# Two transformer blocks in one kernel: attention maps added before they are divided, bias rows of the modulations first, one more weight slot in two expert stages, SSD decays with their step in the exponent

## The reference, cut to what matters

```python
# first block, for layer in (0, 1)
mod = silu(c) @ ada_w[layer] + ada_b[layer]            # shift, scale, gate, twice
h = rms_norm(x, g) * (1 + sc1) + sh1
# layer 0: HGRN branch and differential attention; layer 1: windowed attention
#   differential: a1, a2 = softmax(q1 k1), softmax(q2 k2)
#   y = rms_norm((a1 - lam * a2) @ v) * (1 - lambda_init)
x = x + g1 * y
x = x + g2 * routed_moe(h2, ...)                       # 16 experts, top 2
# second block
acum = cumsum(dt * a)                                  # within chunks of 128 tokens
y_diag = einsum(cb, exp(acum_t - acum_s) * lower, x * dt_s)
states = einsum(bm, exp(acum_end - acum) * dt, x)      # forwards and backwards
y_off = einsum(cm, exp(acum), h_prev)
# then Fourier branch, gates, output product, rms_norm
ffn = expert_choice_ffn(h, ...)                        # 16 experts, 32 tokens each
```

## Time and profile before

| | us |
|---|---|
| median of 3 runs | 2982.18 (2977.14 to 2983.55) |
| the profiled execution | 2980.63 |
| its span in the profile | 2979.2 |

### The profile page before, as it was taken

The page is one execution under the profiler, slowest core; times in us unless marked ns, Lnnn a source line. Parts: engine busy times, 40 slices in busy tenths (PEclk is TensorE's granted clock), DMA queues, the critical chain, the costliest instruction groups (busy, mean ns, idle before and its releaser), DMA issues.

```text
span 2979.2 us, 30705 instructions
## 1 busy us (share of the span) xinstructions
PE 2396.1 (80%) x12449; PEld 1451.7 (49%) x12449; DVE 1295.0 (43%) x2115; ACT 968.8 (33%) x1492; POOL 108.7 (4%) x177
## 2 busy tenths in 40 slices
PE   5967696869999999698487777759888987778776
PEld 3733474658888887443232222228666762222222
DVE  2276638469999998354200000024685351000001
ACT  3344324348888787233100000034234340000000
POOL 1000300010000000100100000000000000000000
PEclk8978798879999999799799999979999998999999
DMA  9267650169999996664699999963103428999997
GB/s 346 93 228 279 204 215 1 58 245 388 395 393 395 392 385 250 242 245 167 225 398 398 401 402 401 406 229 114 57 1 119 171 89 340 409 409 409 409 410 287
DMA packets 246855, 819.48 MB, mean 275 GB/s; under 512 B 11075, under 2 KB 11241, under 8 KB 246448
## 3 DMA queue, kind: packets, MB, share of 16 engines
q1 hardware_dynamic: 226688, 753.88, 65.7%
q0 software_dynamic: 14432, 45.54, 4.5%
q10 hardware_dynamic: 5584, 17.98, 1.5%
HBM read 779.46 MB, written 37.90 MB: 274 GB/s over the span
## 4 chain that ended last, share of the span: by engine, by line
PE 58%; DMA 25%; DVE 10%; issue 3%; ACT 2%; SPq 1%; POOL 1%; DVEq 0%; PEldq 0%; ACTq 0%; POOLq 0%
PE PS L253 55%; DMA ring<-in_moe_w_up 8%; DMA ring<-in_w_e_down 5%; DMA ring<-in_moe_w_gate 4%; DMA ring<-in_w_e_up 3%; DMA ring<-in_w_e_gate 2%; PE PS L1824 1%; DVE hgrn L964 1%; DMA ring<-in_moe_w_down 1%; SPq L390 1%; DMA ring<-in_ada_w 1%; PE PS L566 1%; DVE SM L2460 0%; DMA row<-YP,DST 0%; DMA SM<-in_router_w 0%
## 5 line engine op out<-in xcount | busy, mean ns | idle before, releaser
L426 DVE TENSOR_TENSOR cut<-ring,cut 128x1024 fp32r<-128x1024 f32 x492 | 584.3, 1221 | 261.8 <-ACT cut L418 250.2
L418 ACT CAST cut<-ring 128x1024 fp32r<-128x1024 f32 x492 | 508.8, 1053 | 348.6 <-PE PS L253 321.7
L253 PE MATMUL PS<-cut,xeT 128*128 128x512 f32 x1536 | 366.1, 395 | 3.3 <-DVE cut L426 3.2
L253 PEld LDWEIGHTS PS<-cut,xeT 128*128 128x128 f32 x1536 | 286.7, 189 | 68.3 <-DVE cut L426 6.3
L253 PE MATMUL PS<-ring,hidT 128*64 128x512 f32 (+1 forms) x1024 | 242.4, 623 | 71.2 <-DMA ring<-in_w_e_down 33.5
L253 PE MATMUL PS<-ring,xeT 128*64 128x512 f32 x1024 | 239.0, 614 | 72.4 <-DMA ring<-in_moe_w_gate 38.1
L253 PE MATMUL PS<-ring,XE 128*32 128x512 f32 x1008 | 235.6, 621 | 62.9 <-DMA ring<-in_w_e_up 40.9
L253 PE MATMUL PS<-cut,parts 128*128 128x512 f32 x864 | 210.4, 406 | 24.5 <-DVE cut L426 14.8
L253 PE MATMUL PS<-parts,cut 128*128 128x512 f32 x864 | 204.2, 396 | 3.6 <-DVE cut L426 3.6
L253 PEld LDWEIGHTS PS<-cut,parts 128*128 128x128 f32 x864 | 168.5, 196 | 67.6 <-issue 18.7
L253 PEld LDWEIGHTS PS<-ring,xeT 128*64 128x64 f32 x1024 | 76.2, 140 | 234.0 <-issue 169.8
(11 more groups left out here) (539 smaller groups left out, 2494.0 us busy)
## 6 DMA issues: line engine op xcount, KB each, us to landing
ring<-in_moe_w_gate SPq DMA_DIRECT2D x64, 2048.0 KB, 12.8
ring<-in_moe_w_up SPq DMA_DIRECT2D x64, 2048.0 KB, 12.2
ring<-in_moe_w_down SPq DMA_DIRECT2D x64, 2048.0 KB, 12.2
ring<-in_w_e_up SPq DMA_DIRECT2D x32, 2048.0 KB, 18.6
ring<-in_w_e_down SPq DMA_DIRECT2D x32, 2048.0 KB, 20.0
ring<-in_w_e_gate SPq DMA_DIRECT2D x31, 2048.0 KB, 19.8
ring<-in_ada_w SPq DMA_DIRECT2D x24, 2048.0 KB, 9.2
ring<-in_w_in SPq DMA_DIRECT2D x13, 2048.0 KB, 7.5
```

Of the source, the lines that this page charges most:

```text
L253: return pe.matmul(o, l, r, start=start, stop=stop, **kw)
L418: act.copy(self.bufs[i % len(self.bufs)][0], w).then_inc(self.high.sem, 1)
L426: dve.tensor_tensor(low, w, high.bitcast(F32), ALU.subtract).then_inc(self.low.sem, 1)
```

## The change

Seven edits:

1. **Ring of layer 1:** a ninth slot (number 10). The router's buffers are laid closer together, the fourth wide slot begins at word 5976, and the second output buffer of a block lies where the modulations' inputs (`CP`) were.
2. **Ring of the last experts:** an eighth slot (number 11, at word 9216), ahead of slot 9 in the order. `H` and `hid` move into the rows of `X` that held the context.
3. **Modulations:** the bias product comes first, and for units 0 to 5 the wait for VectorE's copy stands behind it.
4. **Differential attention:** one maximum over both maps; one signal for both score products; the second map is multiplied by a column (sum of the first over sum of the second, times lambda) and added to the undivided first map in one operation; the copy of the finished values (`keep`) becomes a product with the first map's reciprocal, kept per unit in `inv`.
5. **States:** ScalarE copies the first two results and weighs the last two inputs, head by head (2 times 24 operations of 128x64), VectorE weighs the first four up front; TensorE may run up to four operations ahead instead of two; the decay of a state no longer waits for its product.
6. **Within:** identity and mask are copied once to fp32r tiles, and the mask's product uses them; the logarithm of the step (`LD`) goes into the bias, so that VectorE adds the two directions in one operation of 128x256 and multiplies with `CB`.
7. **Convolution:** ScalarE takes the logarithm ahead of the three exponentials in `sums`, VectorE bounds the step from below.

```diff
-    W.place(range(NS), end0, end1, extra=(5, 6, 7), first=moe1 + NS)
+    W.place(range(NS), end0, end1, extra=(5, 6, 7, 10), first=moe1 + NS)
...
-    W.place((3, 4, 8, 9), moe2, end2, once=(9,), going=moe2 - 3)
+    W.place((3, 4, 8, 11, 9), moe2, end2, once=(9,), going=moe2 - 3)
...
-        pe.wait_ge(*mod_taken(u))
+        if u > 5:
+            pe.wait_ge(*mod_taken(u))
         pe.wait_ge(*(mod_in_second(4) if u == 1 else mod_in(mod_loads[u + 1] - 1)))
         if u:
             pe.wait_ge(*mod_done(u - 1))
-        mm(whole[0:12, :], KC[:, C_SUM:C_SUM + 12], sums, True, False)
-        mm(whole[0:12, :], KC[0:6, C_REP:C_REP + 12], br, False, True).then_inc(mod_summed.sem, 1)
+        mm(whole[0:12, :], KC[0:6, C_REP:C_REP + 12], br, True, False)
+        if u < 6:
+            pe.wait_ge(*mod_taken(u))
+        mm(whole[0:12, :], KC[:, C_SUM:C_SUM + 12], sums, False, True).then_inc(mod_summed.sem, 1)
...
-            for m in range(2):
-                dve.wait_ge(*scored(2 * u + m))
-                vs.add(dve.tensor_reduce(st[:, m:m + 1], bank(2 * (u % 2) + m)[:, 0:nk], AX.X, ALU.max))
-            dve.wait_ge(*vs.now)
+            dve.wait_ge(*scored(u))
+            vs.settle(dve.tensor_reduce(st[:, 0:2], two(bank(2 * (u % 2), 2))[:, :, 0:nk], AX.X, ALU.max))
...
-            vs.settle(dve.reciprocal(st[:, 4:6], st[:, 2:4]))
-            vs.settle(dve.tensor_scalar(a1, a1, st[:, 5:6], lam, ALU.mult, ALU.mult))
-            dve.scalar_tensor_tensor(out=a0, in0=a0, scalar=st[:, 4:5], in1=a1,
+            vs.settle(dve.reciprocal(inv[:, 2 * u:2 * u + 2], st[:, 2:4]))
+            vs.settle(dve.tensor_scalar(st[:, 5:6], inv[:, 2 * u + 1:2 * u + 2], st[:, 2:3], lam, ALU.mult, ALU.mult))
+            dve.scalar_tensor_tensor(out=a0, in0=a1, scalar=st[:, 5:6], in1=a0,
                                      op0=ALU.mult, op1=ALU.add).then_inc(mixed.sem, 1)
...
-                dve.tensor_copy(YB[:, u // 4, :], bank(6 + u // 4 % 2)).then_inc(y_taken.sem, 1)
+                first = inv[:, 2 * u - 6:2 * u + 2].rearrange("p (h m) -> p h m", m=2)[:, :, 0:1]
+                dve.tensor_tensor(h4(YB[:, u // 4, :]), h4(bank(6 + u // 4 % 2)), first.to_broadcast([P, 4, P]),
+                                  ALU.mult).then_inc(y_taken.sem, 1)
...
-            yo = [room("yo", 512, 5120 + 512 * i) for i in range(2)]
+            yo = [room("yo", 512, 5120), tile("yo", 512, CP0)]
...
-        for i in range(3):
-            wide_slots[5 + i] = room("ring", SLOT, ROOM - (3 - i) * SLOT)
+        for i, n in enumerate((5, 6, 7, 10)):
+            wide_slots[n] = room("ring", SLOT, ROOM - (4 - i) * SLOT)
...
                 act.wait_ge(*sums_taken(0))
+                act.activation(LD, LD, ACT.Ln)
                 act.activation(ET, bank(6)[:, 192:384], ACT.Exp)
...
-                vs.settle(dve.tensor_scalar(NA, AC, -1.0, None, ALU.mult))
+                vs.settle(dve.tensor_tensor(NA, LD, AC, ALU.subtract))
...
+        dve.tensor_scalar(LD, DT, 1e-30, None, ALU.max)
...
             if k > 1:
-                pe.wait_ge(*op_taken(k - 2))
+                pe.wait_ge(*(first_taken(k - 2) if k < 4 else op_taken(k - 4)))
             if way == "to":
-                pe.wait_ge(*weighted(n))
+                pe.wait_ge(*(weighted(n) if n < 4 else late_weighted(n - 4)))
...
+    def states_scalar():
+        act.copy(unit_mask, ident)
+        act.copy(far_mask, KC[:, C_NF:C_NF + 2 * P])
+        for k, (_, d, c, _) in enumerate(STATES[0:2]):
+            act.wait_ge(*op_made(k))
+            for g in range(4):
+                ins = act.copy(HS[d][:, g * 384:(g + 1) * 384], bank(4 * k, 4)[:, g * 512:g * 512 + 384])
+            ins.then_inc(first_taken.sem, 1)
+        for n in (4, 5):
+            _, d, c, _ = STATES[into[n]]
+            act.wait_ge(*op_made(into[n - 2]))
+            for h in range(24):
+                col = c * 48 + d * 24 + h
+                ins = act.mul(XWs[n % 2][:, 64 * h:64 * h + 64], XH[:, c, 64 * h:64 * h + 64], WS[:, col:col + 1])
+            ins.then_inc(late_weighted.sem, 1)
...
-        weigh(0)
-        weigh(1)
-        for k, (way, d, c, first) in enumerate(STATES):
+        for n in range(4):
+            weigh(n)
+        for k, (way, d, c, first) in list(enumerate(STATES))[2:]:
...
-            mm(two(bank(v % 3)), ident, KC[:, C_NF:C_NF + 2 * P].unsqueeze(1).to_broadcast([P, 2, 2 * P]), True, False)
+            mm(two(bank(v % 3)), unit_mask, far_mask.unsqueeze(1).to_broadcast([P, 2, 2 * P]), True, False)
...
-            for hh in range(2):
-                cf = c * 48 + 2 * u + hh
-                vs.add(dve.tensor_scalar(ww[:, hh * P:(hh + 1) * P], dd[:, hh * 256:hh * 256 + P], DT[:, cf:cf + 1], None, ALU.mult))
-            dve.wait_ge(*vs.now)
-            for hh in range(2):
-                cf = c * 48 + 2 * u + hh
-                wv = ww[:, hh * P:(hh + 1) * P]
-                vs.add(dve.scalar_tensor_tensor(out=wv, in0=dd[:, hh * 256 + P:hh * 256 + 256], scalar=DT[:, cf + 24:cf + 25],
-                                                in1=wv, op0=ALU.mult, op1=ALU.add))
-            dve.wait_ge(*vs.now)
+            both = dd.rearrange("p (h d t) -> p h d t", h=2, d=2)
+            vs.settle(dve.tensor_tensor(two(ww), both[:, :, 0, :], both[:, :, 1, :], ALU.add))
```

More of the change, by code:

```diff
@@ L1578, in routed @@
         rw3 = chunked(rw, 8)
-        parts = room("logit_parts", 512, 8192)[:, 0:nch * P]
+        parts = room("logit_parts", nch * P, 2 * nch * D)
         v3 = lambda a: a.rearrange("p (c e) -> p c e", e=16)
@@ L2827, in program @@
     weighted, op_made, op_taken = S.new("weighted", "dve"), S.new("op_made", "pe"), S.new("op_taken", "dve")
+    first_taken, late_weighted = S.new("first_taken", "act"), S.new("late_weighted", "act")
+    unit_mask, far_mask = tile("unit_mask", P, CP0, F32R), tile("far_mask", 2 * P, CP0 + P, F32R)
+    into = [k for k, op in enumerate(STATES) if op[0] == "to"]
     shares = XWs[1]
```

71 lines of the change are left out of this document (34 added, 37 removed).

## The result

The changed kernel takes 2940.11 us in the median of 4 runs (2939.05 to 2947.30), beside 2979.86 us (2977.14 to 2983.55) for the kernel before on the same chip: ratio 0.9871, 95% interval 0.9850 to 0.9891. The forecast was 2942. The profiled execution after took 2940.46 us (span 2939.0), against 2980.63 before: 40.2 us less, where the sum said 40.0.

What follows compares the result with a forecast made beforehand. No single resource was taken as the bound: DMA in the two expert streams, VectorE in attention and states, TensorE in within. Terms summed to -40.0 us from 2980.6, giving 2940.6, forecast 2942; eight-in-ten range 2933 to 2958.

Steps and rivals of the forecast that it cites:

- Rings: Streams of layer 1 and the last experts: one more piece sent before each restart, -5.5 and -5.2 us.
- The rival in which the piece is hidden: Both rings: the extra transfers run into other traffic and give 0; 2953 us, chance 0.04.
- Modulations: Front stage: bias product covers VectorE's copy, -0.8 us; units 2 to 5 together -0.3.
- Attention: Differential attention: column operations replace map scalings and maxima are united; 6.1 us less VectorE time, -4.7 taken.
- States: States stage: VectorE loses two weighings and two sets of copies, 7.4 us; -6.5 after replaying the waits.
- Within: Within stage: cheaper fp32r mask product, 24 units 16.5 us; chunk ends -0.7 each, starts +0.9; together -17.
- Convolution: Convolution: ScalarE's added logarithm and table load, about 1.7 us, are covered: nothing; +1.7 if uncovered.
- Half in the stages: Rival: new waits between three engines leave within 9, states 3, attention 2.5; -26.3 us, 2956, chance 0.19.
- The clock rival: Within: lighter units let TensorE's clock fall throughout, +20 instead of -17 us; 2979, chance 0.03.
- The product not being cheaper: Within rival: fp32r between fp32 products might not run faster; within gives 1.4, 2958 us, chance 0.05.
- surplus block: Expert stages rival: new roundings send one token more, so `more` runs once; +58 us, 3000, chance 0.02.
- the prediction's signs: Expected: mask product one record of about 0.23 us, unit about 1.5, states near 45, attention near 54, unchanged DMA rates.

Runs made afterwards that it cites:

- experiment 5: Changed kernel with only the placing of the pieces as before, one slot fewer in each of the two streams: 2957.03 us.
- experiment 6: Changed kernel with two slots fewer in each of the two streams: 2965.97 us in one run.
- experiment 11: Changed kernel with the modulations in the old order and the mask product issued twice in each within unit: 2947.47 us in one run.
- experiment 7: Changed kernel with differential attention as before (both maps scaled, separate maxima, plain copy of the values): 2952.72 us in one run.
- experiment 4: Changed kernel with the states as before: VectorE weighs all six inputs and takes the first two products: 2952.76 us in one run.
- experiment 3: Changed kernel with ScalarE's late inputs in 96 operations instead of 48, plus a second logarithm and exponential in the convolution: 2953.54 us in one run.
- experiment 12: Changed kernel with each within exponential of 128 columns made as two of 64: 2945.16 us in one run.
- experiment 1: Changed kernel with only the mask product back in fp32: 2960.88 us.
- experiment 8: Changed kernel with the mask laid out 512 wide instead of 256 words read twice: 2944.62 us.
- experiment 2: Changed kernel with VectorE's old five operations a within unit and no logarithm, fp32r mask product kept: 2949.68 us.

## Why the prediction was right

- **Rings (-5.5, -5.2).** Right in mechanism and size: 5.2 and 5.25 in the traces, 5.1 and 5.5 in experiment 5, a line in experiment 6. The rival in which the piece is hidden is out. That the start of the last stream was read 0.4 us too late did not change the size.
- **Modulations (-0.8, -0.3).** The front's term measured 0.9 at either level of the clock (experiment 11). The 0.3 of the later units can't be seen: the end of HGRN lies between 2.5 us earlier and 4.8 us later in kernels with the same code up to there.
- **Attention (-4.7).** The mis-sized term. The column's operation was costed at 169 ns and takes 272, 16 x 0.10 = 1.6 us; the stage gave 3.2 (experiment 7 and the two traces, all at the same clock level), inside the bounds -2 to -6.5. The union of the maxima was as costed: a pair of 256 keys takes 0.72 us to the next start in place of 0.78.
- **States (-6.5).** 6.6 in the traces, 5.7 to 6.1 in experiment 4. The narrow operation cost the 0.24 us of the earlier trace rows; VectorE has the one wait of 1.03 us for the second "from" product that the replay gave. The slack of ScalarE was read too wide: 0.26 us an operation is the limit, not 0.31 (experiment 3). By the Trainium skill (VectorE: DVE Perf Modes, the section on the TRN2 errata) an operation was an estimated 0.24 us, and the trace agrees with 0.241 from SBUF. For a source in PSUM the same table has 172 in place of 224 cycles, an estimated 0.197 us for this width, and experiment 12 shows 0.205.
- **Within (-17).** 17.4, from terms that erred both ways. The mask product takes 0.31 us and not 0.23, so a unit gave 0.63 and 24 units 15.1, not 16.5 (experiments 1, 8 and 11). The chunks' ends gave 0.7 each beyond it, as costed (4.02 against 5.32 us, and 8.27 against 9.58, of each 0.6 the mask product). The starts, put down as a loss of 0.9, gave 0.9: with the shorter wait at the end of chunk 0 the clock did not fall. Before, the next chunk's mask product takes 1.91 us and its unit 3.15; after, 0.47 and 1.12 (2186.04, 2187.16, 2188.28). This is the price of the low clock that the prediction named as a rival, here on the good side. Experiment 1 gives its size: with the fp32 mask product but VectorE's short end (a wait of 0.87 us), the clock stays up, and chunk 1 takes 23.74 us to its last mask product where it took 25.40 before, 1.7 less. The forecast loss came as well and is hidden in the net: in chunk 1 TensorE waits 0.77 us for VectorE (at 2191.54), and to its last mask product the chunk takes 17.78 us, 1.0 more than experiment 1's 23.74 less eleven units' gain of 0.63. What the sum did not say is that the two halves need each other (experiment 2): with VectorE's five operations the product's gain would have been 7.7 us.
- **Convolution (0).** Right: the stretch did not change (128.62 to 128.58 us), and the cover is at least 3.3 us (experiment 3).
- **The rivals.** Half in the stages did not come: TensorE keeps the last place, ScalarE is busy 1.15 us of a unit's 1.57. Experiment 12 shows how near it was: 0.5 us more on ScalarE costs 8.5 us of the stage. The clock rival did not come either, granted clock 0.93 in the stage. The product not being cheaper is out (0.31 against 0.92 us, experiment 1), and there was no surplus block (the page counts 64 pieces of each expert weight, as before). Of the prediction's signs the mask product came as one record, but of 0.47 us and not about 0.23. By the Trainium skill (TensorE: Matmul & The Clock Gate, HAM oscillation) gaps between groups bring the low clock back; experiments 2 and 12 agree at the end of chunk 0, where, over three waits of 0.5 to 0.9 us in a row, the products fell to the low level. The changed kernel's one wait of 0.86 us did not bring it back.

The total agrees better than its terms, and that part is luck: attention was 1.5 too high, within 0.4 too low, the front's clock gave 1.3 that no term held, and the shifts outside the stages of the table, between 0.9 lost and 1.0 gained, nearly cancel. And the median of the changed kernel is less sure than the one set of runs says: the eight executions give 2943.8, still in the range.

## What to carry to other kernels

Price an edit in a pipelined loop at its steady unit and at its ends apart: an engine that falls a little behind in each unit is invisible in the middle while buffers cover it, and is paid for, with the clock on top, where the chain drains (experiment 2). Two engines near the same limit can make their edits worth together more than the sum (7.7 and 3.3 apart, 17.4 together). In the two streams bound by DMA here, a slot that can be filled before the restart is worth just one piece's time, for one slot and for two.

## What the runs showed of the hardware

- A fp32r product of 128x512 among fp32 products holds TensorE 0.31 us, behind another of its kind 0.23 to 0.24; in fp32 it holds it 0.92 us and shows two records.
- On ScalarE, back to back, a scaled copy within SBUF costs 0.241 us for 64 columns and 0.21 for 32, an exponential from PSUM 0.205 us for 64 columns and 0.28 for 128: half the columns, 32 for 64, saved only 0.03 us.
- On VectorE an operation on two columns with constants costs 169 ns, one on a single column 220 with one pointer and a second tensor and 272 with two pointers.
- Identical code shows two lengths in a stage (50.5 us in attention where its first 10 us have a granted clock of 0.67, 49.4 where they have 0.9; 3.69 or 1.98 us for four products of the modulations, about the ratio of TensorE's 1.2 and 2.4 GHz), and the eight executions of the changed kernel fall in two groups some 7 us apart. A gain of 2 us can't be read from two profiles of the whole, only from the stage and with the clock's level beside it.
